# A stick-breaking attention in which the slices of the gates' projection are placed by each step's own columns, not by a fixed period

## The chip, the cores and the metric

One core of a Trainium2 chip runs the whole program. The metric is the device time of one execution in microseconds (us). Engines by their short names: TensorE is PE, VectorE is DVE, ScalarE is ACT, GpSimd is POOL, SyncE is SP (here it only issues transfers).

## What is computed

One inference step of a hybrid decoder for two groups: a prompt of 1024 tokens and 8 samples of 8 tokens each with 256 cached ones. A retention layer comes first, then shared keys and values, then one layer of stick-breaking attention with 16 heads of 64, whose part of the reference is:

```
def sb_layer(h, pos, k_all, v_all, k_pos, w_in, q_g, bias, w_out):
    q, g = jnp.split(h @ w_in, 2, axis=-1)
    q = rmsnorm(q.reshape(B, L, SB_HEADS, SB_DH), q_g)
    o = stick_breaking(q, k_all, v_all, pos, k_pos, bias).reshape(B, L, SB_W)
    return (jax.nn.silu(g) * o) @ w_out

# inside stick_breaking, for each block of 128 queries
z = jnp.einsum('bqhd,bkhd->bhqk', qi, k).astype(F32) * scale + bias_f
log_keep = jnp.where(mask, jax.nn.log_sigmoid(-z), 0.0)
tail = lax.cumsum(log_keep, axis=3, reverse=True)
w = jnp.where(mask, jnp.exp(jax.nn.log_sigmoid(z) + tail_excl), 0.0)
out = jnp.einsum('bhqk,bkhd->bqhd', w, v)
```

The gate g needs a product of its own, `h @ w_in` for 1024 columns. Half of it is made before attention, the other half (columns 512 to 1023) during it. That second half is what the change moves.

## The kernel before

The program has stages that follow each other: opening, retention heads, the product behind them, shared keys and values with queries, attention, output. The change touches the function `attention` alone.

**Pieces.** Heads go in 8 pairs, a pair's queries in 8 blocks of 128. Each of these 64 units is cut into pieces of at most 512 columns of keys (of one head, or of both where 256 columns or fewer are left); 8 further pieces belong to the sample group, one for each sample. That makes 168 pieces, `NPC`; `HALF` is 80, half of the 160 without samples.

**Steps.** Every engine runs its own loop over the pieces p = 0 to 167, a step each. PE in step p: the score of piece p+1 into one of two banks of `z` (L1785, L1786; it waits until the second sigmoid of piece p-1 is done, semaphore `sticks`), then slices (first half of the step), the transposes of piece p-3 (L1795), the attends of the pieces that `batches` lists for this step (L1821), then slices again (second half). ACT in step p: two sigmoids of piece p, `pa_keep` and `pa_take` (L1932), a copy of the transposed piece p-3 for two pieces in three (L1943), and, where a tile of gates ends in step p, the tile's sigmoid, `open_gates` (L1977), for which it waits. DVE: the scan of piece p-1 (L2044), every third copy (L2053), the gate of finished units, and a tile's last product, `finish_gates` (L2122). POOL: the multiplication of piece p (L1722), and two steps after the end of a tile its store, `store_gates` (L1702).

**Slices.** The half product has nine tiles: eight for the prompt and tile 8 for the samples. Each has eight slices of three matmuls with 512 columns (L2980 to L2982; two, L3002 and L3003, for the samples), 72 in all, all into the one bank `pa_acc`. So a tile's first slice waits until DVE has finished the tile before it (`g_ready`). How many slices are done before each half of a step is said by `slices_before(p, part)`: five before the loop, one more in each of the first steps, and from step 4 on eight in six steps (12 halves) of every eight, none in the last two:

```
if p < FIRST_SLOT:
    return min(KD, START + p + (part > 0))
q = 2 * (p - FIRST_SLOT) + (part > 0)
return min(SLICES, KD + KD * (q // PERIOD) + min(KD, (q % PERIOD) * KD // FILL))
```

**What hangs on the end of the tiles.** `steps_done_at(p)` lists the tiles that end in step p, and `G_END` is the step in which tile 8 ends. From it come the opening of the sample gates (PE turns them at G_END+2, DVE copies them at G_END+3, POOL stores them in its step G_END+2), POOL's clearing of `sa_q_diag` at G_END+3 and, on SP at step G_END+1, `load_samples`: the page table, eight loads of the samples' inputs (three of new rows, head rows, bias, `hidden`, two masks; semaphore `inputs_s`), then the first pages of keys and values.

**What does not hang on it.** PE turns the samples' new queries in step 74 (`new_slots` begins at HALF-6) and waits there for all eight inputs (L1748). SP loads the gates of pair 4, `load_g(4)` (L1623), in its step 67, since `g_slots` counts from the end of a pair:

```
def load_g(pair):
    if pair >= 2:
        sp.wait_ge(stored[pair % 2], 16 * (pair // 2))
    if pair == PAIRS // 2:
        for n in range(2):
            sp.wait_ge(g_stored[n], 16 * len(range(n, NT, 2)))
```

Pairs 4 to 7 use the columns that the slices make, so pair 4 waits for the stores of all nine tiles. SP works through its steps in order, and whatever it waits for holds back all that stands behind.

Of the kernel before, what the change touches and what calls it, by code (L numbers as in the profile page):

```python
# [23 lines left out]
P = 128  # L24
D = 1024
KD = D // P
# [64 lines left out]
def build_program(nc, t_in, t_out):  # L91
    ctx = ExitStack()
    with ctx:
        persist = Persistent(nc, ctx, t_in)
        banks = ExitStack()
        at = nc.sbuf_base
        with ExitStack() as joined:
            hw_sem, rt_sem, ro_sem, kq_sem = semaphores(nc, joined, "hw", "rt", "ro", "kq")
            with ExitStack() as layer:
                h = Modulated(nc, layer)  # L100
                head = HeadWeights(nc, hw_sem("w_loaded"))
                opening(nc, t_in, persist, h, head)
                block = joined.enter_context(nc.Block(no_gpsimd_drain=True))
                first = FirstWeights(nc, "ro", t_in["ret_w_out"][0], H * DV // P)
                ahead = RetainedAhead(nc, at, banks.enter_context(nc.psum_tensor("rt_acc", [P, 2, NB], F32)), first)
                kept = retention_heads(nc, t_in, t_out, persist, h, head, first, ahead, block, rt_sem)
            late = ExitStack()
            late_sem = semaphores(nc, late, "pa")
            with ExitStack() as middle:
                pairs = PairBuffers(nc)  # L110
                rated = middle.enter_context(nc.sbuf_tensor("rated", [P, 3, NT], F32))
                x = middle.enter_context(nc.sbuf_tensor("x", [P, NT, D], F32))
                proj = Projection(nc)
                kq_stored = [late_sem(name) for name in ("kq_stored0", "kq_stored1", "kq_last_stored", "kq_parts0", "kq_parts1", "kq_parts_k")]
                with banks:
                    handed = retained_out(nc, t_in, persist, first, x, rated, proj, ahead, kept, block, ro_sem)
                shared_kv_and_queries(nc, t_in, t_out, persist, x, rated, proj, pairs, kq_stored, handed, block, kq_sem)
        first = FirstWeights(nc, "ao", t_in["sb_w_out"][0], KD)
        sa = SampleBuffers(nc, proj.kept)
        held = Held(nc, sa, pairs, ctx.enter_context(nc.psum_tensor("z", [P, 2, NB], F32)))  # L120
        attention(nc, t_in, t_out, persist, proj, first, sa, held, pairs, kq_stored, late, late_sem)
        output(nc, t_in, t_out, persist, first, sa, held)
# [1254 lines left out]
def attention(nc, t_in, t_out, ps, proj, first, sa, held, pairs, kq_stored, ctx, sem):  # L1377


    with ctx:  # L1380
# [11 lines left out]
        pieces = []  # L1392
        for u in range(UNITS):
            wide = (where(u)[1] + 1) * P
            spans = [(NB, wide - NB), (0, NB)] if wide > NB else [(0, wide)]
# [3 lines left out]
        HALF = len(pieces) // 2  # L1399
        at = HALF + 13 - 9  # L1400
# [5 lines left out]
        NPC = len(pieces)  # L1406
# [42 lines left out]
        LAG, TR, WR, KR = 3, 5, 5, 3  # L1449
# [50 lines left out]


        SLICES = NT * KD
        START, FIRST_SLOT, PERIOD, FILL = KD - 3, 4, 16, 12

        def slices_before(p, part):

            if p < FIRST_SLOT:
                return min(KD, START + p + (part > 0))
            q = 2 * (p - FIRST_SLOT) + (part > 0)
            return min(SLICES, KD + KD * (q // PERIOD) + min(KD, (q % PERIOD) * KD // FILL))  # L1510

        def steps_done_at(p):

            begun = slices_before(p, 0) if p else 0
            return [t for t in range(NT) if begun < (t + 1) * KD <= slices_before(p + 1, 0)]
# [60 lines left out]
            else:  # L1576
                engine.wait_ge(w_taken_a, len([n for n in range(p + 1) if not on_vector(n)]))

        batches, held_back = {}, []
        for p, at in enumerate(pieces):  # L1580
            if at.b is not None and held_back:
                batches[held_back[-1] + LAG + 1] = held_back
                held_back = []
            if at.closes:
                held_back = held_back + [p]
            if at.b is not None or len(held_back) == (2 if p < HALF else 1) or at.closes and at.last and at.u % 4 == 3:
                batches[p + LAG + 1] = held_back
                held_back = []
        attend_step = {p: step for step, batch in batches.items() for p in batch}
        gate_step = {attend_step[ends[u]] + 1: u for u in range(3, UNITS, 4)}  # L1590
        assert len(attend_step) == sums_done(NPC - 1) and len(gate_step) == UNITS // 4
# [148 lines left out]
        def _(pe):  # L1740
# [134 lines left out]
            for p in range(NPC):  # L1875
                if p + 1 < NPC:
                    score(p + 1)
                if p in new_slots:
                    turn_new(new_slots[p])
                if p in page_slots:  # L1880
                    turn_pages(*page_slots[p])
                project(slices_before(p, 0), slices_before(p, 1))
                if p >= LAG:
                    turn_w(p - LAG)
                for q in batches.get(p, ()):
                    attend(q)
                project(slices_before(p, 1), slices_before(p + 1, 0))
                if p == G_END + 2:
                    turn_gates()
                if sample_before(p, LAG + 3) is not None:  # L1890
                    fold(sample_before(p, LAG + 3))
# [1365 lines left out]
```

## Time and profile before

| | |
|---|---|
| median of 3 runs | 1812.44 us (1810.49 to 1814.74) |
| the profiled execution | 1811.87 us, its span in the trace 1810.2 us |
| PE busy | 1758.1 us, 97% of the span |
| DVE, ACT, POOL busy | 969.4, 778.2, 267.0 us |
| granted PE clock, mean of the span | 0.995 |
| attention, from its first score to its last | 1362.6 to 1700.4 us |

The table's rows are shares of one profiled execution. PE's busy time counts each matmul to its modelled end, so it overlaps a little with what follows; the clock is given as a share of 2.4 GHz. Where an engine's idle time ends, the trace names the instruction that released it.

### The profile page before, as it was taken

The numbers are of one execution on the slowest core, as the hardware profiler recorded it, in microseconds if no ns is written. First come the engines' busy times: TensorE is split into PE (matmuls) and PEld (weight loads), VectorE is DVE, ScalarE is ACT, GpSimd is POOL, SyncE is SP. The second block draws the span as 40 slices with busy tenths as digits, with TensorE's granted clock in tenths as the row PEclk, the third lists the DMA queues.
The fourth block names the chain that finished last, engine by engine and source line by source line (L and its number), as shares of the span: only waits on it lengthen the run. The fifth ranks groups of instructions, "written<-read, shape, count | busy, mean of one in ns | idle before, by whom it ended". The sixth has DMA issues, their size and how long they took to land. (4 is left out here: it accounts for less than half of the span.)

```text
span 1810.2 us, 27358 instructions
## 1 busy us (share of the span) xinstructions
PE 1758.1 (97%) x9783; PEld 1388.7 (77%) x9783; DVE 969.4 (54%) x1867; ACT 778.2 (43%) x1683; POOL 267.0 (15%) x324
## 2 busy tenths in 40 slices
PE   5999999999999999999999999999998998999998
PEld 2678787878787878777788877788887777677677
DVE  4653535454444444453645554676625667777762
ACT  3742323232323232331434433353326768888720
POOL 2000000000000000000000011101113545555300
PEclk9999999999999999999999999999999999999999
DMA  9231312122222222366433578423365449696252
GB/s 338 87 97 60 95 61 89 67 79 76 75 80 68 87 61 93 104 209 217 130 84 116 190 231 271 157 80 112 102 186 134 123 117 251 194 236 190 86 192 93
DMA packets 153898, 240.60 MB, mean 133 GB/s; under 512 B 13289, under 2 KB 102177, under 8 KB 152770
## 3 DMA queue, kind: packets, MB, share of 16 engines
q1 hardware_dynamic: 136778, 179.69, 33.5%
q0 software_dynamic: 17024, 59.66, 9.3%
q8 instruction: 57, 0.93, 0.2%
q14 instruction: 39, 0.31, 0.1%
HBM read 177.91 MB, written 61.42 MB: 132 GB/s over the span
## 5 line engine op out<-in xcount | busy, mean ns | idle before, releaser
L488 PE MATMUL rt_acc<-rt_w_hi,rt_h_hi 128*128 128x512 f32 x504 | 203.3, 403 | 1.0 <-DVE rt_h_lo L1030 1.0
L490 PE MATMUL rt_acc<-rt_w_hi,rt_h_lo 128*128 128x512 f32 x504 | 197.1, 391 | 0.0
L489 PE MATMUL rt_acc<-rt_w_lo,rt_h_hi 128*128 128x512 f32 x504 | 196.5, 390 | 0.0
L1722 POOL TENSOR_TENSOR pa_take<-pa_take,pa_after_key 128x512 f32<-128x512 f32 (+2 forms) x152 | 153.3, 1011 | 141.7 <-DVE pa_after_key L2044 137.8
L1073 DVE TENSOR_TENSOR rt_by_cos<-rt_raw,rt_cos 128x256 f32<-128x256 f32 (+1 forms) x72 | 30.5, 424 | 243.9 <-ACT rt_raw L903 243.9
L914 ACT COPY rt_qk_t<-rt_tr 128x256 f32<-128x256 f32 (+1 forms) x72 | 26.0, 361 | 278.4 <-PE rt_tr L722 278.4
L2992 PE MATMUL kq_acc<-kq_w_hi,kq_h 128*128 128x512 f32 x320 | 128.6, 402 | 0.0
L2995 PE MATMUL kq_acc<-kq_w_hi,kq_h 128*128 128x512 f32 x320 | 125.1, 391 | 0.0
L2993 PE MATMUL kq_acc<-kq_w_lo,kq_h 128*128 128x512 f32 x320 | 124.7, 390 | 0.0
L1932 ACT ACTIVATE pa_keep<-z,pa_bias 128x128 f32<-128x128 f32 (+3 forms) x192 | 111.1, 600 | 5.9 <-PE z L1786 5.7
L1932 ACT ACTIVATE pa_take<-z,pa_bias 128x128 f32<-128x128 f32 (+3 forms) x192 | 111.1, 603 | 0.0
L490 PEld LDWEIGHTS rt_acc<-rt_w_hi,rt_h_lo 128*128 128x128 f32 x504 | 94.6, 188 | 20.6
L488 PEld LDWEIGHTS rt_acc<-rt_w_hi,rt_h_hi 128*128 128x128 f32 x504 | 94.8, 188 | 19.1 <-DVE rt_h_lo L1030 1.4
L489 PEld LDWEIGHTS rt_acc<-rt_w_lo,rt_h_hi 128*128 128x128 f32 x504 | 94.9, 188 | 17.9 <-issue 0.2
L780 PE MATMUL rt_acc_g<-rt_h_hi,rt_g_hi 128*128 128x512 f32 x256 | 105.6, 413 | 0.0
L2044 DVE TENSOR_TENSOR_SCAN pa_after_key<-pa_keep,pa_eye 128x384 f32<-128x384 f32 (+3 forms) x112 | 93.2, 850 | 19.5 <-POOL pa_take L1722 8.5
L782 PE MATMUL rt_acc_g<-rt_h_lo,rt_g_hi 128*128 128x512 f32 x256 | 100.1, 391 | 0.0
L781 PE MATMUL rt_acc_g<-rt_h_hi,rt_g_lo 128*128 128x512 f32 x256 | 100.1, 391 | 0.0
L1795 PE MATMUL pa_wt<-ident,pa_take 128*128 128x128 f32 x592 | 93.1, 275 | 2.6 <-POOL pa_take L1722 1.4
L1785 PE MATMUL z<-pa_k_t,pa_q_hi 128*128 128x128 f32 (+3 forms) x192 | 76.4, 406 | 16.0 <-ACT pa_take L1932 12.5
L1795 PEld LDWEIGHTS pa_wt<-ident,pa_take 128*128 128x128 f32 x592 | 70.9, 140 | 22.1 <-POOL pa_take L1722 6.7
L2044 DVE TENSOR_TENSOR_SCAN pa_after_key<-pa_keep,pa_after_key,pa_eye 128x512 f32<-128x512 f32 x64 | 81.7, 1276 | 7.4 <-ACT pa_keep L1932 4.0
(406 smaller groups left out, 4025.8 us busy)
## 6 DMA issues: line engine op xcount, KB each, us to landing
ro_a_raw<-retained SPq DMA_DIRECT2D x14, 1024.0 KB, 6.0
rt_w_raw<-in_ret_w_in SPq DMA_DIRECT2D x16, 512.0 KB, 5.2
rt_w_raw<-in_ret_w_in SPq DMA_DIRECT2D x8, 1024.0 KB, 7.8
rt_old<-in_state_ret SPq DMA_DIRECT2D x8, 1024.0 KB, 5.9
rt_g_raw<-in_ret_w_in SPq DMA_DIRECT2D x8, 1024.0 KB, 5.2
out_st_sample<-rt_new POOLq DMA_DIRECT2D x8, 1024.0 KB, 7.9
k_cols<-kq_parts POOLq DMA_DIRECT2D x16, 512.0 KB, 4.0
kq_w_raw<-in_sb_w_in SPq DMA_DIRECT2D x4, 2048.0 KB, 10.2
```

Of the source, the lines that this page charges most:

```text
L488: nc.tensor.matmul(dst, h_hi[:, k, cols], w_hi[:, k, :], start=k == 0, stop=False)
L489: nc.tensor.matmul(dst, h_hi[:, k, cols], w_lo[:, k, :], start=False, stop=False)
L490: last = nc.tensor.matmul(dst, h_lo[:, k, cols], w_hi[:, k, :], start=False, stop=k == KD - 1)
L780: nc.tensor.matmul(dst, g_hi[:, k, part], h_hi[:, k, cols], start=k == 0, stop=False)
L781: nc.tensor.matmul(dst, g_lo[:, k, part], h_hi[:, k, cols], start=False, stop=False)
L1722: nc.gpsimd.tensor_tensor(own, own, later, ALU.mult).then_inc(weighed, 1)
L1795: last = nc.tensor.transpose(dst[:, b * P:(b + 1) * P], take(p)[:, b * P:(b + 1) * P], ps.ident[:])
L1932: last = nc.scalar.activation(dst[:, cols], z[:, p % 2, cols], ACT.Sigmoid, scale=(2 * part - 1) * DH ** -0.5, bias=shift)
L2044: nc.vector.tensor_tensor_scan(ring[:, c0:c0 + n][:, ::-1], k[:, ::-1], opening, seed, ALU.mult, join).then_inc(scanned, 1)
L2992: nc.tensor.matmul(dst, hi, w_hi, start=k == 0, stop=False)
L2993: last = nc.tensor.matmul(dst, hi, w_lo, start=False, stop=t == NPT and k == KD - 1)
L2995: last = nc.tensor.matmul(dst, proj.lo(t)[:, k, :], w_hi, start=False, stop=k == KD - 1)
```

## The change

The constants of the period go. A new function, `spread_slices`, makes a list `cuts` of how many slices are done before each half step, and `slices_before` reads it. For each step it adds up columns: `own_work` is what PE has of its own (the next score, the transposes, the attends, with a charge of 110 for each round of them), `fed_work` what ACT has (two sigmoids of each scan at nine quarters a column, with rounds). A slice counts 690. In a step's second half as many slices are due as keep PE's sum in proportion to ACT's; in its first half one, if any is due by then. At most two are laid in a half, never past the end of a tile, and for three halves after a tile's end none (`PAUSE`). All are done by step 69 (`LEVEL` is 70). The table `batches` is computed earlier, since `own_work` reads it; its rule is the same.

```
-        START, FIRST_SLOT, PERIOD, FILL = KD - 3, 4, 16, 12
+        START, PAUSE, LEVEL = KD - 3, 3, 7 * HALF // 8
+        ROUND, SHARE = 110, 690
...
+        def own_work(p):
+
+            work = 0
+            if p + 1 < NPC:
+                work += ROUND + 7 * pieces[p + 1].wide // 8
+            if p >= LAG:
+                work += 7 * pieces[p - LAG].wide // 8
+            spans = [pieces[q].n // P for q in batches.get(p, ()) if pieces[q].b is None]
+            return work + sum(2 * P * n * 7 // 8 for n in spans) + (2 * ROUND if spans else 0)
+
+        def fed_work(p):
+
+            return 2 * ROUND * pieces[p].scans + 9 * pieces[p].wide // 4 + ROUND
+
+        fed = [sum(fed_work(q) for q in range(p + 1)) for p in range(LEVEL)]
+        owned_by = [sum(own_work(q) for q in range(p + 1)) for p in range(LEVEL)]
+        to_spread = owned_by[-1] + SHARE * (SLICES - START)
+
+        def spread_slices():
+
+            cuts, done, free_at = [START], START, 0
+            for p in range(LEVEL):
+                for part in range(2):
...
+                    goal = START + (fed[p] * to_spread // fed[-1] - owned_by[p]) // SHARE if part else done + 1
+                    if part == 0 and START + (fed[p] * to_spread // fed[-1] - owned_by[p]) // SHARE <= done:
+                        goal = done
+                    goal = SLICES if p == LEVEL - 1 and part else goal
+                    edge = (done // KD + 1) * KD
+                    if 2 * p + part < free_at:
+                        goal = done
+                    goal = max(done, min(goal, done + 2, edge, SLICES))
+                    if goal == edge and goal > done:
+                        free_at = 2 * p + part + 1 + PAUSE
+                    done = goal
+                    cuts.append(done)
+            return cuts
+
+        cuts = spread_slices()

         def slices_before(p, part):

-            if p < FIRST_SLOT:
-                return min(KD, START + p + (part > 0))
-            q = 2 * (p - FIRST_SLOT) + (part > 0)
-            return min(SLICES, KD + KD * (q // PERIOD) + min(KD, (q % PERIOD) * KD // FILL))
+            return cuts[min(2 * p + (part > 0), len(cuts) - 1)]
```

Worked out from the two rules, for steps 1 to 73:

| | before | after |
|---|---|---|
| tile 0 to 8 ends in step (1: first half, 2: second half) | 2 (1), 9 (2), 17 (2), 25 (2), 33 (2), 41 (2), 49 (2), 57 (2), 65 (2) | 1 (2), 7 (1), 16 (1), 25 (1), 33 (2), 44 (1), 51 (1), 61 (1), 69 (2) |
| steps without slices and without attends | 3, 10, 11, 18, 26, 35, 42, 50, 51, 58, 66, 68, 69, 70, 72, 73 | 2, 8, 17, 24, 26, 32, 60, 62, 70, 72, 73 |
| steps with attends and without slices | 19, 27, 34, 43, 59, 67, 71 | 12, 15, 19, 23, 31, 34, 37, 41, 43, 45, 49, 52, 55, 59, 67, 71 |
| `G_END` | 65 | 69 |

The line numbers of the function's later parts grow by 37 in the changed kernel (L1785 becomes L1822, L2980 becomes L3017).

The order on PE, steps 10 and 11 (`z` rows are a score, `pa_acc` rows a slice, `pa_wt` rows the transposes). Before, from the score of piece 11 that opens step 10 to the score that opens step 12:

```order
L1785 MATMUL z<-pa_k_t_3429,pa_q_hi_3430 128x512
L1786 MATMUL z<-pa_k_t_3429,pa_q_lo_3434 128x512
L1795 MATMUL pa_wt<-ident,pa_take 128x128 x4
L1785 MATMUL z<-pa_k_t_3429,pa_q_hi_3430 128x384
L1786 MATMUL z<-pa_k_t_3429,pa_q_lo_3434 128x384
L1795 MATMUL pa_wt<-ident,pa_take 128x128 x4
L1785 MATMUL z<-pa_k_t_3429,pa_q_hi_3430 128x384
L1786 MATMUL z<-pa_k_t_3429,pa_q_lo_3434 128x384
```

After, from the same score to the one that opens step 11:

```order
L1822 MATMUL z<-pa_k_t_3429,pa_q_hi_3430 128x512
L1823 MATMUL z<-pa_k_t_3429,pa_q_lo_3434 128x512
L3017 MATMUL pa_acc<-kq_h,kq_w_hi_3439 128x512
L3018 MATMUL pa_acc<-kq_h,kq_w_lo_3440 128x512
L3019 MATMUL pa_acc<-kq_h,kq_w_hi_3439 128x512
L1832 MATMUL pa_wt<-ident,pa_take 128x128 x4
L3017 MATMUL pa_acc<-kq_h,kq_w_hi_3439 128x512
L3018 MATMUL pa_acc<-kq_h,kq_w_lo_3440 128x512
L3019 MATMUL pa_acc<-kq_h,kq_w_hi_3439 128x512
L1822 MATMUL z<-pa_k_t_3429,pa_q_hi_3430 128x384
L1823 MATMUL z<-pa_k_t_3429,pa_q_lo_3434 128x384
```

Step 10 had no slice and has two now, one before its transposes and one behind them; step 11, whose score is the last pair of rows, had none either and has one.

The order on SP, around the loads that its steps 64 to 70 issue (`pa_v` is `load_v(4)`, `pa_g_t` is `load_g(4)`, `sa_pages` to `sa_by_group` are the page table and the eight input loads of `load_samples`). Before:

```order
L1615 DMA pa_v<-out_v_prompt 128x8x128
L1626 DMA sa_pages<-in_page_table 1x16
L1629 DMA sa_new_rows<-q_rows 64x1024
L1629 DMA sa_new_rows<-out_k_sample 64x1024
L1629 DMA sa_new_rows<-out_v_sample 64x1024
L1630 DMA pa_head_rows<-in_head_rows 16x128
L1631 DMA sa_bias_col<-in_sb_bias 16x1
L1633 DMA sa_hidden<-in_hidden_s 128x1024
L1633 DMA sa_own_block<-in_own_block 128x4
L1633 DMA sa_by_group<-in_by_group 128x32
```

and behind the last page of values, before the loads of the next pair:

```order
L1303 DMA sa_v_pages<-in_cache_v 128x1024
L1623 DMA pa_g_t<-g_cols 128x1024
L1342 DMA pa_k_t<-k_cols 64x1024
L1343 DMA pa_q_hi<-q_cols 64x1024
L1344 DMA pa_q_lo<-q_cols 64x1024
```

After:

```order
L1652 DMA pa_v<-out_v_prompt 128x8x128
L1660 DMA pa_g_t<-g_cols 128x1024
L1663 DMA sa_pages<-in_page_table 1x16
L1666 DMA sa_new_rows<-q_rows 64x1024
L1666 DMA sa_new_rows<-out_k_sample 64x1024
L1666 DMA sa_new_rows<-out_v_sample 64x1024
L1667 DMA pa_head_rows<-in_head_rows 16x128
L1668 DMA sa_bias_col<-in_sb_bias 16x1
L1670 DMA sa_hidden<-in_hidden_s 128x1024
L1670 DMA sa_own_block<-in_own_block 128x4
L1670 DMA sa_by_group<-in_by_group 128x32
```

`load_g(4)` stood behind the whole of `load_samples`, pages included; it stands ahead of it now, because `load_samples` moved from step 66 to step 70 and `load_g(4)` stayed in step 67. The other orders on SP are unchanged.

## Rows read from the trace of the kernel before

**Rows 1.** The page's table of busy time: us, share of the span, instructions.

```profile
PE 1758.1 (97%) x9783; PEld 1388.7 (77%) x9783; DVE 969.4 (54%) x1867; ACT 778.2 (43%) x1683; POOL 267.0 (15%) x324
```

**Rows 2.** Windows of attention: start to end, length, then the header's columns.

```profile
core 0: us, PE busy (x) PEld busy (x) DVE busy (x) ACT busy (x) POOL busy (x), PEclk, DMA share, GB/s
1362.60:1366.50 3.90, 3.90 (x13) 3.13 (x14) 1.36 (x6) 2.43 (x5) 0.31 (x1) 0.57 0.65 214
...
1373.30:1508.20 134.90, 127.69 (x986) 104.19 (x987) 90.65 (x107) 96.34 (x194) 68.91 (x73) 1.00 0.55 130
1508.20:1531.00 22.80, 19.35 (x177) 15.04 (x176) 17.92 (x22) 18.98 (x39) 13.45 (x14) 1.00 1.02 325
```

**Rows 3.** Waits of PE, 1372 to 1500: us, times, longest.

```profile
PE z L1785 <- ACT pa_take L1932: 7.9, 9, 1.1
```

**Rows 4.** Waits of ACT, 1372 to 1500.

```profile
ACT pa_g_out L1977 <- PE pa_acc L2982: 7.4, 6, 2.2
```

**Rows 5.** Timeline of PE, steps 8 to 11: start, us, operation, [idle before].

```profile
1382.49 0.60 PE L1795 MATMUL pa_wt<-ident,pa_take 128*128 128x128 f32 x4
1382.85 0.48 PE L1785 MATMUL z<-pa_k_t,pa_q_hi 128*128 128x512 f32 x1
...
1384.40 1.75 PE L1821 MATMUL pa_out<-pa_w_t,pa_v 128*64 128x128 f32 x28
...
1386.65 0.39 PE L2982 MATMUL pa_acc<-kq_h,kq_w_hi 128*128 128x512 f32 x1
...
1387.34 0.60 PE L1795 MATMUL pa_wt<-ident,pa_take 128*128 128x128 f32 x4
1388.88 0.45 PE L1785 MATMUL z<-pa_k_t,pa_q_hi 128*128 128x384 f32 x1 [0.95 <-ACT pa_take L1932]
```

**Rows 6.** Timeline of PE, steps 65 to 74.

```profile
1507.98 0.40 PE L3003 MATMUL pa_acc<-kq_w_lo,kq_h_s 128*128 128x512 f32 x1
...
1511.69 0.39 PE L1785 MATMUL z<-pa_k_t,pa_q_hi 128*128 128x256 f32 x1 [2.33 <-ACT pa_take L1932]
...
1517.77 0.33 PE L1785 MATMUL z<-pa_k_t,pa_q_hi 128*128 128x128 f32 x1 [0.84 <-ACT pa_take L1932]
...
1524.46 0.71 PE L1748 MATMUL pa_wt<-ident,sa_new_rows 64*128 64x64 f32 x8
```

**Rows 7.** Timeline of SP's issues, from `load_samples` to `load_g(4)`.

```profile
1508.41 0.24 SPq L1626 DMA_DIRECT2D sa_pages<-in_page_table  x1
...
1512.50 0.43 SPq L1633 DMA_DIRECT2D sa_by_group<-in_by_group  x1
...
1520.75 1.42 SPq L1303 DMA_DIRECT2D sa_v_pages<-in_cache_v  x2
1523.97 0.34 SPq L1623 DMA_DIRECT2D pa_g_t<-g_cols  x1
```

**Rows 8.** Timeline of DVE, the copy of the turned sample gates.

```profile
1515.25 0.40 DVE L2126 COPY pa_g_out<-pa_acc 128x256 f32<-128x256 f32 x1
```

**Rows 9.** Timeline of POOL, the store of the sample gates.

```profile
1516.71 0.81 POOL L1702 DMA_DIRECT2D g_cols<-pa_g_out  x1
```

**Rows 10.** Transfers issued 1516 to 1517.5: count, KB each, us to landing.

```profile
sa_v_pages<-in_cache_v SPq DMA_DIRECT2D x2, 512.0 KB, 8.1
g_cols<-pa_g_out POOLq DMA_DIRECT2D x1, 128.0 KB, 7.2
```

**Rows 11.** Transfers issued 1481 to 1482.5, a quiet time.

```profile
g_cols<-pa_g_out POOLq DMA_DIRECT2D x1, 256.0 KB, 2.4
```

**Rows 12.** Transfers issued 1508 to 1513.5, the last of the inputs.

```profile
sa_by_group<-in_by_group SPq DMA_DIRECT2D x1, 16.0 KB, 6.8
```

**Rows 13.** Timeline of PE, the first scores and slices of attention.

```profile
1362.59 0.30 PE L1785 MATMUL z<-pa_k_t,pa_q_hi 128*128 128x128 f32 x1 [2.96 <-PEq L57]
...
1363.47 0.63 PE L2981 MATMUL pa_acc<-kq_h,kq_w_lo 128*128 128x512 f32 x1
1363.90 0.63 PE L2982 MATMUL pa_acc<-kq_h,kq_w_hi 128*128 128x512 f32 x1
...
1366.75 0.39 PE L2980 MATMUL pa_acc<-kq_h,kq_w_hi 128*128 128x512 f32 x1
```

More of the change, by code:

```diff
@@ L1502, in attention @@
         SLICES = NT * KD
-        START, FIRST_SLOT, PERIOD, FILL = KD - 3, 4, 16, 12
+        START, PAUSE, LEVEL = KD - 3, 3, 7 * HALF // 8
+        ROUND, SHARE = 110, 690
+        batches, held_back = {}, []
+        for p, at in enumerate(pieces):
+            if at.b is not None and held_back:
+                batches[held_back[-1] + LAG + 1] = held_back
+                held_back = []
+            if at.closes:
+                held_back = held_back + [p]
+            if at.b is not None or len(held_back) == (2 if p < HALF else 1) or at.closes and at.last and at.u % 4 == 3:
+                batches[p + LAG + 1] = held_back
+                held_back = []
@@ new lines, in attention @@
+        fed = [sum(fed_work(q) for q in range(p + 1)) for p in range(LEVEL)]
[5 more added lines that the diff above has]
+                for part in range(2):
+                    behind = owned_by[p - 1] if p and not part else owned_by[p] if part else 0
+                    goal = START + (fed[p] * to_spread // fed[-1] - owned_by[p]) // SHARE if part else done + 1
[11 more added lines that the diff above has]
+            return cuts
@@ L1577, in wait_taken @@
                 engine.wait_ge(w_taken_a, len([n for n in range(p + 1) if not on_vector(n)]))
[L1579 to L1588, printed above, removed]
         attend_step = {p: step for step, batch in batches.items() for p in batch}
```

## The prediction, made before the changed kernel was run

> **What bounds the kernel now.** I read the busy table of the page first. TensorE (PE) is busy for 97% of the span [rows 1], so a change of order can give back only its idle time. The stretches of attention come next. Steps 4 to 65, which carry the gates' slices, last 134.9 us with PE busy 127.7 of them; the 22.8 us behind them, in which the slices have ended and the sample group is being opened, are worse covered, 19.35 us [rows 2]. The list of waits says what PE waits for while slices run: in steps 4 to 60 it is one thing, 9 times, the second sigmoid of a piece (`pa_take`) on ScalarE (ACT), 7.9 us in all and at most 1.1 [rows 3]. Score of piece p+1 may not start before the sigmoids of piece p-1 have left `z`.
>
> Where do the nine stand? The timeline at the end of tile 1 shows it. Attends of step 9 run for 1.7 us from 1384.40, then comes the tile's last slice, whose last matmul starts at 1386.65. ACT has to open that tile before its next sticks, so it stands until then; six such waits cost it 7.4 us [rows 4]. PE meanwhile enters steps 10 and 11, which hold neither a slice nor attends, only a score and four transposes. It runs through the first faster than ACT through two sigmoids, and waits 0.95 us before the score that opens step 11 [rows 5], and again behind that. I call such a step bare. From the table of steps in the text on the change, the order of before has ten bare steps among 3 to 60 and nine of them are followed by a wait. The matmul before a wait is drawn to its modelled end (0.60 us from 1387.34, for four transposes; the same four from 1382.49 let the next score in after 0.36 [rows 5]), so a wait costs PE 0.24 more than its number: 7.9 + 9 x 0.24 = **10.1 us** for nine.
>
> **The change, term by term.** Each of the 72 slices is still done once, with the same instructions, and no engine gets work that it had not. Only their place changes, so these are the terms.
>
> *1. Waits between slices.* After the change the bare steps among 2 to 62 are 2, 8, 17, 24, 26, 32, 60 and 62: eight, not ten. The pairs 10, 11 and 50, 51 are gone. Six of nine tiles now end in a step's first half, ahead of transposes that ACT waits for anyway, so ACT's 7.4 us of standing shrinks too. That is not what decides, since a bare step is short for ACT whatever came before it. By the rate of before (nine waits for ten bare steps, 10.1 / 9 = 1.12 us each) eight bare steps give 8 x 0.9 x 1.12 = 8.1 us: gain 2.0 us. Bounds: none of it, or all 10.1 us. I take the rate, as it is the nearest.
>
> *2. Steps 66 to 69.* Before, the last slice is in step 65; steps 66, 68 and 69 are bare. PE waits 2.33 us behind step 66, because ACT stands in the opening of the sample tile, and 0.84 behind step 69 [rows 6]. Now the slices reach to step 69. The 2.33 moves with the sample tile's end to step 70; the 0.84 (1.1 with the 0.24) goes. Gain 1.1 us.
>
> *3. The sample inputs are late.* This is the largest term, and it lies on SP, not on PE. SP issues `load_samples` at step `G_END + 1`, where G_END is the step that ends tile 8. It moves from step 66 to step 70. `load_g(4)` stays at step 67, and for this pair alone it waits until all nine gate stores have landed, the one of tile 8 too. Before, it stood behind the sample loads, and its wait until 1523.97 stopped nobody [rows 7]. Now it stands in front of them: the order on SP shows `pa_g_t` directly ahead of `sa_pages`. PE's first transpose of the sample rows stays in step 74 and waits for all eight input loads.
> Take M as the end of the last slice (before: its last matmul starts at 1507.98 [rows 6], M = 1508.2). The chain from M: merge, sigmoid, transposes, and VectorE's (DVE) copy of the turned gates, which starts 1515.25 and takes 0.40 [rows 8]; GpSimd (POOL) issues the store at 1516.71, M + 8.5 [rows 9]. It landed after 7.2 us, while SP was sending for pages [rows 7, 10]; an earlier store of gates in a quiet time landed after 2.4 [rows 11]. Now SP has nothing under way then, so I take 2.4 and keep 7.2 as the far end: M + 10.9. Then SP issues `load_g(4)`, 0.5 us with its queue: M + 11.4. From the first sample load (1508.41) to the issue of the last input (1512.50) are 4.1 us [rows 7], and this last landed after 6.8 [rows 12]: 10.9 in all, so the inputs are there at **M + 22.3**; with a landing of 2.4 instead of 6.8 at M + 17.9.
> When does PE want them? From the start of step 70 (1517.77) to the first sample transpose (1524.46) PE goes 6.7 us without waiting [rows 6]. With the 2.33 + 0.24 of term 2 it is there at M + 9.3. So it waits 22.3 - 9.3 = **13.0 us**. Ends: 17.9 - 9.3 = 8.6, and 13.0 + 4.8 = 17.8 if the store takes 7.2 again. Nothing covers this: everything behind step 74 on PE is queued behind the wait, DVE and ACT need the turned pieces, and POOL needs DVE. When it ends, the others have caught up, but the short waits of the sample opening behind it hang on chains that start at that transpose.
>
> *4. The clock after the pause.* The granted clock falls where PE has stood. Before attention it stands for 2.96 us; then two neighbouring matmuls of the first slices start 0.43 us apart (1363.47, 1363.90), against 0.23 from 1366.75 on [rows 13], and the mean clock of that stretch reads 0.57 [rows 2]: 1.2 GHz for most of it. From 1363.06, where they begin, to 1366.75 are nine matmuls, so some 8 x 0.2 = 1.6 us were lost. A pause four times as long should bring the same once: cost 1.6 us; ends 0 (steps 75 to 77 already wait for ACT and DVE) and 3.2 for twice that.
>
> **Sum:** -2.0 - 1.1 + 13.0 + 1.6 = +11.5 us. The profiled execution took 1811.87 us (span 1810.2), so 1823.4; the median of the runs is 0.57 above it, and 1811.87 + 11.5 + 0.57 gives **1824.0 us**.
>
> The Trainium skill speaks on the store in term 3 ("DMA: Bandwidth & Descriptors", Specifications): pieces under 512 bytes don't run at line rate, because the engine reads and rewrites. The sample gates' store has rows of 64 numbers, 256 bytes, while the quiet store that I priced it by has rows of 2 KB. By that page the 2.4 us would be too little; with the far end of 7.2 the sum would be 16.3 and the time 1828.8. The row alone, 7.2 us, doesn't part the size of the pieces from the traffic.
> On the clock the skill ("TensorE: Matmul & The Clock Gate", Why this matters for your kernels) advises against idle gaps between bursts, and this speaks against the change. Rows 13 agree; the sum would be the same by rule and by row.
>
> **Rivals.**
> *A. Even spreading takes away all of ACT's waits.* Every step would then be longer than ACT's two sigmoids and a copy. For it: PE's work in these steps exceeds ACT's on average (127.7 against 96.3 us busy [rows 2]). Against it: eight bare steps are left. It gives -10.1 - 1.1 + 13.0 + 1.6 = +3.4 us, 1815.8. Chance 0.05, within the measurement's 0.2% (3.6 us, about what a measurement of this kernel can tell from no change).
> *B. Faster.* The loads of the samples are not late: either SP passes the wait of `load_g(4)` early, or PE reaches the transposes after the inputs. It decides if the inputs are there before M + 9.3. Then terms 3 and 4 vanish: -3.1 us, 1809.3; with A's full gain 1801.2. For it: before, PE never waited for an input there. Against it: the store that SP now waits for is not even issued before M + 8.5 by rows 8 and 9. Chance 0.03.
> *C. More is late.* The store takes its 7.2 us and the clock needs twice as long: -3.1 + 17.8 + 3.2 = +17.9, 1830.3; the key pages, issued behind the inputs, might add a wait in step 78. SP issues the pages right behind the inputs, and PE has four steps to do before it turns them, so I price none. Chance 0.07.
> *D. Nothing moves in time* because the order is only arithmetic on the same work. The ordered lists speak against it. It is in the 0.05 of A.
>
> **How the numbers follow.** Forecast 0.85, A (with D) 0.05, B 0.03, C 0.07. The forecast's own ends: 8.6 us of wait, 3.1 gained and no loss by the clock give +5.5, 1817.9; 17.8 with 1.6 and 3.1 gives +16.3, 1828.8. The range 1817 to 1830 takes in both and most of C. Faster by over 0.2% has B's 0.03, within 0.2% A's 0.05, slower the other 0.92.
>
> **What would show it.** SP issues `pa_g_t` before `sa_pages`, some 3 us after POOL's last `g_cols` (term 3's first half). PE shows one wait of 9 to 18 us before the first transpose of `sa_new_rows`, the longest of attention. The clock reads half behind it. Between steps 4 and 62 PE's waits for `pa_take` add up to 6 to 8 us, against 7.9. From step 80 on the steps last as before. It would be wrong if that one wait is under 5 us, or if the waits for `pa_take` fall under 2 us.

## The result, and the profile after

The changed kernel takes 1823.78 us, median of five runs (1822.44 to 1827.83), against 1810.58 for the kernel before (five runs, 1810.49 to 1814.74). The ratio is 1.0066, 95% interval 1.0049 to 1.0083: 8.9 to 15.0 us slower. The forecast was 1824.0, range 1817 to 1830.

The profiled execution has a span of 1823.0 us against 1810.2, a difference of 12.8. From its page, the span and the busy table:

```profile
span 1823.0 us, 27358 instructions
...
PE 1761.5 (97%) x9783; PEld 1392.7 (76%) x9783; DVE 969.9 (53%) x1867; ACT 777.2 (43%) x1683; POOL 266.8 (15%) x324
```

The instructions and the 97% are those of [rows 1]. The busy time of PE grew by 3.4 us with as many matmuls, so some of them ran slower; the rest of the 12.8 is idle time. Below are PE's waits over attention's slices and the opening of the samples (1362 to 1560): total us, times, longest. The kernel before has no entry like the second:

```profile
PE z L1822 <- ACT pa_take L1969: 11.6, 12, 2.4
PE pa_wt L1785 <- DMA sa_by_group<-in_by_group: 11.6, 1, 11.6
```

Who held that load back stands in SP's waits and issues of the same stretch. The waits of SP, and then its timeline (L1659 is the wait in `load_g(4)` for the gate stores, L1652 a load of values, L1663 to L1670 `load_samples`):

```profile
SPq L1659 <- DMA g_cols<-pa_g_out: 23.9, 1, 23.9
```

```profile
1501.34 0.39 SPq L1652 DMA_DIRECT2D pa_v<-out_v_prompt  x1
1525.70 0.33 SPq L1660 DMA_DIRECT2D pa_g_t<-g_cols  x1
1526.07 0.29 SPq L1663 DMA_DIRECT2D sa_pages<-in_page_table  x1
...
1530.20 0.43 SPq L1670 DMA_DIRECT2D sa_by_group<-in_by_group  x1
```

SP stands for 23.9 us and issues nothing between 1501.34 and 1525.70. The nine loads of the samples need no gates at all, yet they are issued behind the wait. The first one leaves at 1526.07, against 1508.41 before [rows 7]. The wait ends with the store of tile 8, in POOL's timeline and in the list of transfers issued from 1522 to 1534 (KB each, us to landing):

```profile
1523.20 0.81 POOL L1739 DMA_DIRECT2D g_cols<-pa_g_out  x1 [3.33 <-DVE pa_g_out L2163]
```

```profile
g_cols<-pa_g_out POOLq DMA_DIRECT2D x1, 128.0 KB, 2.4
...
sa_by_group<-in_by_group SPq DMA_DIRECT2D x1, 16.0 KB, 4.8
```

PE's timeline from the last slice to step 77 shows what became of these 12 us:

```profile
1512.07 0.40 PE L3040 MATMUL pa_acc<-kq_w_lo,kq_h_s 128*128 128x512 f32 x1
...
1515.90 0.50 PE L1822 MATMUL z<-pa_k_t,pa_q_hi 128*128 128x512 f32 x1 [2.42 <-ACT pa_take L1969]
...
1517.45 2.91 PE L1858 MATMUL pa_out<-pa_w_t,pa_v 128*64 128x128 f32 x28
...
1535.05 1.11 PE L1785 MATMUL pa_wt<-ident,sa_new_rows 64*128 64x64 f32 x8 [11.55 <-DMA sa_by_group<-in_by_group]
...
1543.23 0.39 PE L1822 MATMUL z<-pa_k_t,pa_q_hi 128*128 128x256 f32 x1
```

The same pieces of before, for comparison: the score that opens step 71, its attends, and the score in step 77.

```profile
1518.93 0.50 PE L1785 MATMUL z<-pa_k_t,pa_q_hi 128*128 128x512 f32 x1
...
1520.03 1.75 PE L1821 MATMUL pa_out<-pa_w_t,pa_v 128*64 128x128 f32 x28
...
1530.30 0.39 PE L1785 MATMUL z<-pa_k_t,pa_q_hi 128*128 128x256 f32 x1
```

The 28 matmuls of step 71's attends are the same work in both, and take 2.91 us instead of 1.75. The windows of the three parts (steps 71 to 73, the wait, and the steps behind it) show the granted clock, PEclk, in the last column but two:

```profile
core 0: us, PE busy (x) PEld busy (x) DVE busy (x) ACT busy (x) POOL busy (x), PEclk, DMA share, GB/s
1515.90:1523.30 7.40, 7.38 (x52) 5.93 (x52) 4.26 (x7) 4.98 (x12) 2.88 (x4) 0.77 0.00 0
1523.30:1535.00 11.70, 0.20 (x1) 0.00 (x0) 3.29 (x3) 1.23 (x3) 5.64 (x5) 0.65 0.77 207
1535.00:1543.20 8.20, 7.92 (x56) 6.12 (x56) 1.46 (x2) 4.15 (x8) 0.00 (x0) 0.67 1.03 408
```

Means between 0.5 and 1.0 say that half clock (1.2 GHz) held for a part of each. There are two stretches of it, one from just behind PE's pause of 2.42 us, one that begins within the pause of 11.55 and goes on behind it. Laid along PE's timeline, the 12.8 us of the span are:

| stretch | before | after | difference |
|---|---|---|---|
| start to attention's first score | 1362.59 | 1361.62 | -1.0 |
| first score to the start of step 71 | 156.34 | 154.28 | -2.1 |
| steps 71 to 73, to the first sample transpose or the wait | 5.53 | 7.43 | +1.9 |
| the wait for the sample inputs | 0 | 11.7 | +11.7 |
| from there to the score in step 77 | 5.84 | 8.18 | +2.3 |
| the rest, to the end | | | about 0 |

The first line is code that the change doesn't touch. In the thirteen profiles of this study attention's first score began anywhere between 1360.34 and 1363.19, so a difference of 1 us there says nothing. The second line is firmer: three further profiles with the slices of the change (experiments 1 and 3 and the busy wait of 4) took 154.3 to 154.4 us there. The fourth, the change itself in experiment 4, took 155.7; its mean clock over 1362 to 1373 was 0.69, where the others have 0.84 to 0.89.

### The profile page after: what moved, and what is told of

It reads as the page before. It is cut to its first block and busy times, and to the rows that moved or that the text cites. A ratio compares the mean times of both kernels' runs of the same rounds, so it can differ in the third digit from the quotient of the medians.

```text
span 1823.0 us, 27358 instructions
## 1 busy us (share of the span) xinstructions
PE 1761.5 (97%) x9783; PEld 1392.7 (76%) x9783; DVE 969.9 (53%) x1867; ACT 777.2 (43%) x1683; POOL 266.8 (15%) x324
## 5 line engine op out<-in xcount | busy, mean ns | idle before, releaser
L1822 PE MATMUL z<-pa_k_t,pa_q_hi 128*128 128x128 f32 (+3 forms) x192 | 77.8, 414 | 15.9 <-ACT pa_take L1969 12.6
```

## The experiments

Each kernel differs from the changed kernel or from the one before by one constant or a few lines. Times are medians; a ratio is against the kernel before in runs beside it, its 95% interval in brackets, and a difference in us is that ratio taken of 1810.6. `M` is the end of the last slice, the gates of pair 4 are what `load_g(4)` loads, and a bare step is one without slices and without attends.

**1. Only SP's order put back.** In the changed kernel, `load_g(4)` moves from step 67 to step 71, so it stands behind `load_samples` again:

```
-            g_slots = {ends[NPT * pair - 1] + 8: pair + 1 for pair in range(1, PAIRS - 1)}
+            g_slots = {ends[NPT * pair - 1] + (12 if pair == 3 else 8): pair + 1 for pair in range(1, PAIRS - 1)}
```

> The change with one edit: SP loads the gates of pair 4 at step 71 in place of 67, so behind the sample loads of step 70, as it was before. My theory (the one wait of 11.6 us comes from SP standing in load_g(4) ahead of the sample loads): the first sample load is issued 0.2 us after the last slice, the inputs land 9 to 11 us after it, PE asks for them after 9.3 to 11, so the wait falls to under 2 us and the half clock behind it goes: 1823.8 - 11.7 - 2.3 plus 0 to 1.8, that is 1809.8 to 1811.6 us. Rival (the loads are late because they start at step 70 at all, or are slow by themselves): a wait of 6 us or more stays, over 1816 us.

Measured: 1812.02 us, ratio 1.0000 (0.9990 to 1.0009). SP and PE in their timelines:

```profile
1511.84 0.24 SPq L1663 DMA_DIRECT2D sa_pages<-in_page_table  x1
...
1530.77 0.33 SPq L1660 DMA_DIRECT2D pa_g_t<-g_cols  x1
```

```profile
1523.93 0.71 PE L1785 MATMUL pa_wt<-ident,sa_new_rows 64*128 64x64 f32 x8
```

The first sample load is issued 0.2 us behind M, and the first sample transpose has no wait in front. The slices lie as in the change, and the loss is gone: it came from one position in SP's list. Against the kernel before, the new places of the slices are worth nothing that can be measured here. Half clock still came twice, behind a pause of 2.41 us and in steps 77 to 79, where PE had no late input to wait for. There it took 11.63 us from the first sample transpose to that of the key pages, where the kernel before took 10.08. PE's timeline and the window:

```profile
1531.71 1.09 PE L1832 MATMUL pa_wt<-ident,pa_take 128*128 128x128 f32 x4 [1.21 <-DVE sa_bias L2098]
```

```profile
1531.70:1535.00 3.30, 3.29 (x24) 2.70 (x24) 2.19 (x5) 2.06 (x5) 1.26 (x2) 0.50 0.53 159
```

The kernel before has a pause of 1.20 us in the same place and keeps the full clock.

**2. Only SP's order of the change, in the kernel before.** The same line with `6` for pair 3 puts `load_g(4)` ahead of `load_samples`; the slices stay as they were.

> The kernel before with one edit: SP loads the gates of pair 4 at step 65, ahead of the sample loads of step 66; no slice moves. My theory: the store of tile 8 is issued 8.5 us after the last slice (1508.2) and lands 2.4 later, the first sample load then at 1519.5, the last input there at 1519.5 + 4.1 + 4.9 = 1528.5, PE asks at 1524.5: a wait of 4 us before the first transpose of sa_new_rows, and up to 1.6 us of half clock: 1810.6 + 4 to 5.6, 1814.6 to 1816.2 us. Rival (what costs is the place of the slices, not the order on SP): no such wait, 1810.6 us.

Measured: 1818.74 us, ratio 1.0032 (1.0021 to 1.0044), +5.8 us. PE's waits from 1362 to 1560, and SP's timeline:

```profile
PE pa_wt L1748 <- DMA sa_by_group<-in_by_group: 2.9, 1, 2.9
```

```profile
1520.14 0.33 SPq L1623 DMA_DIRECT2D pa_g_t<-g_cols  x1
1520.51 0.29 SPq L1626 DMA_DIRECT2D sa_pages<-in_page_table  x1
```

The swap alone makes the wait, but a short one. `load_g(4)` leaves at M + 11.6, against M + 13.4 in the change, and here PE has steps 66 to 73 to do behind the last slice, and in the change only 70 to 73. So the loss of the change needs both halves: the swap on SP, and an end of the slices four steps nearer to step 74. The time is longer than the 1814.6 to 1816.2 expected, because half clock came twice: behind a pause of 2.35 us, and again from 1.2 us behind the end of the wait. The second time cost as much as in experiment 1 (11.63 us for 10.08), where there is no such wait, so it isn't shown that the wait of 2.9 us brought it.

**3. PE kept busy while it waits.** In the change, 110 transposes of the identity matrix are issued ahead of the wait for the inputs, into columns that the next transposes overwrite. They add work and change nothing of the result.

```
-                if n == 0:
-                    pe.wait_ge(inputs_s, 16 * 8)
...
+                if n == 0:
+                    for _ in range(110):
+                        nc.tensor.transpose(dst[:, 0:P], ps.ident[:], ps.ident[:])
+                    pe.wait_ge(inputs_s, 16 * 8)
```

> The change with 110 transposes of the identity put before PE's wait for the sample inputs, into the bank that the next transposes write anyway. They fill about 9.7 of the 11.7 us in which PE stood. My theory (the 2.3 us lost between steps 74 and 77 is the half clock behind the pause): the wait shrinks to about 2 us, the clock stays full behind it, and the time falls by 2.3 us against the change, to 1821.5. Rival (those steps are slow for another reason, such as transfers or the other engines' queues running dry): they still take 8.2 us, and the time stays at 1823.8.

Measured: 1825.71 us (ratio 1.0072, 1.0056 to 1.0089). PE's timeline, then the window behind the wait:

```profile
1524.95 12.17 PE L1783 MATMUL pa_wt<-ident 128*128 128x128 f32 x110
1538.10 0.71 PE L1787 MATMUL pa_wt<-ident,sa_new_rows 64*128 64x64 f32 x8 [0.97 <-DMA sa_by_group<-in_by_group]
```

```profile
1538.10:1545.80 7.70, 6.34 (x60) 4.85 (x60) 3.20 (x7) 5.59 (x11) 1.46 (x2) 1.00 1.03 407
```

The clock reads 1.00 behind the busy wait. From the first sample transpose to that of the key pages it is 10.08 us, as in the kernel before, against 12.42 in the change: the 2.3 us behind the wait are the clock. But the whole was no faster, and the 1821.5 us expected were missed. The store of tile 8 landed after 3.2 us instead of 2.4, the last input after 5.5 instead of 4.8, and the part behind attention's last score is 0.9 us longer.

**4. The same two again, side by side.** The change as it is:

> The changed kernel once more, unedited, beside the next run on the same chip. It tells how far two profiles of one kernel differ in the chain behind the last slice: the sample inputs at 22 to 24 us after it, the first transpose of sa_new_rows to the first transpose of key pages in 12.4 us (10.1 with full clock), 1823 to 1825 us in all.

and the busy wait:

> The run with 110 transposes in the wait once more, now beside the change itself. In its first run the steps behind the wait took 10.1 us in place of 12.4, as my theory of the clock says, but the inputs landed 24.2 us after the last slice in place of 22.7, and the attention began 1.6 us later. Theory 1 (those two are chance): inputs at 22 to 24 us as in the run beside it, the time 1 to 2.5 us below it. Theory 2 (PE's transposes slow the transfers down): inputs 1.4 us later than in the run beside it again, and the time within 1 us of it.

Measured: 1825.47 for the change (ratio 1.0071, 1.0054 to 1.0088), 1824.53 for the busy wait (1.0062, 1.0046 to 1.0079). The steps behind the wait took 12.06 and 10.08 us, so that part repeats. The total differs by 0.9 us, just under the 1 to 2.5 expected of the first theory, and the two intervals overlap. Inputs were there at M + 23.9 and M + 23.7, so the later inputs of experiment 3 didn't repeat as a difference. Two smaller things did repeat with the added transposes: the store of tile 8 landed after 3.1 us, against 2.4 beside it, and the end behind attention's last score was 0.7 us longer (110.4 against 109.7 us). Why, no run here shows.

**5. The slices end four steps sooner.** The change with `LEVEL` 66 for 70: the same rule of columns, with all slices done by step 65 as in the kernel before.

> The change with LEVEL 66 in place of 70: the same rule lays the slices, but ends them in step 65 as before, so the sample loads are at step 66, ahead of load_g(4). My theory: no late inputs; bare steps (no slice, no attends) among 2 to 62 are 2, 7, 20, 32, 53 and 58, six in place of ten, and at 1.12 us for nine in ten of them 4 x 0.9 x 1.12 = 4.0 us are gained: 1806.6 us. Rival 1 (the placement by columns gives only what it gave in the change, 2.1 us): 1808.5. Rival 2 (denser slices make another engine or the clock the bound): 1810.6 or more.

Measured: 1806.55 us, ratio 0.9964 (0.9949 to 0.9978), -6.5 us, as expected. PE's waits from 1366 to 1503:

```profile
PE z L1822 <- ACT pa_take L1969: 2.9, 5, 1.3
```

In the kernel before it is 7.9 us in 9 waits there, and 8.5 in 9 in the change. Of steps 2 to 62 six are bare, instead of eight in the change and ten before.

**6 and 7. The period of before with another filling.** `FILL` 12 became 14 (seven of eight steps get slices, and four of steps 2 to 62 are bare) and 10 (five of eight get slices, and fourteen are bare).

> The kernel before with FILL 14 in place of 12: a tile's eight slices lie in seven of eight steps. Bare steps among 2 to 62 are then 3, 11, 35 and 51, four in place of ten; the last slice is in step 66. My theory (a bare step costs PE 0.9 x 1.12 us whatever rule lays the slices): 6 x 1.0 = 6 us gained, 1804.6 us. Rival (the waits follow the ends of tiles, where ACT stands for a last slice; there are as many of them as before): within 1 us of 1810.6.

> The kernel before with FILL 10 in place of 12: slices in five steps, none in three. Bare steps among 2 to 62 are 3, 10, 11, 17, 18, 25, 26, 33, 35, 42, 50, 51, 57 and 58, fourteen in place of ten. My theory: 4 x 1.0 = 4 us lost, 1814.6 us. Rival (waits follow the ends of tiles): within 1 us of 1810.6.

Measured: 1807.72 (ratio 0.9971, 0.9959 to 0.9982) and 1814.98 (1.0018, 1.0008 to 1.0027): -5.2 and +3.3 us, where -6 and +4 were expected. So `FILL` 14, one constant of the old rule, can't be told apart from `LEVEL` 66 of the new one: the intervals overlap. PE's waits from 1366 to 1503, first for 14, then for 10:

```profile
PE z L1785 <- ACT pa_take L1932: 4.8, 7, 1.1
```

```profile
PE z L1785 <- ACT pa_take L1932: 7.3, 10, 0.9
```

The sign is that of the count of bare steps both times: six fewer bring 5.2 us, four more cost 3.3. But the waits don't carry the second result. At 10 they list 7.3 us (and 0.8 for POOL), no more than the 7.9 of before, and the kernel is slower all the same, by 3.5 us up to the first sample transpose. Part of it is a stretch at half clock behind a pause of 2.20 us, which the kernel before doesn't have (shown in the last section); the rest stands in no list. And at 14 there are seven waits for four bare steps, so waits stand behind steps with work of their own as well.

**8. `LEVEL` 68.** Six bare steps; the slices end in step 66, so `load_samples` is in step 67, still ahead of `load_g(4)`.

> The change with LEVEL 68 in place of 70: the last slice is in step 66, first half, so the sample loads are in SP's step 67, where they still stand ahead of load_g(4). Six bare steps among 2 to 62 (2, 7, 13, 20, 32, 58), and one fewer behind them. My theory: no late inputs, 4.0 us gained in 2 to 62 and up to 1 behind: 1805.6 to 1806.6 us. Rival (a later end of the slices makes the inputs late in any order on SP): 1810 us or more.

Measured: 1805.12 us (1804.08 to 1805.28), ratio 0.9959 (0.9945 to 0.9973), -7.4 us, 0.5 below the range expected. It is faster than the kernel before and than the change. PE's waits from 1366 to 1503, then its timeline where the other kernels have the pause of 2.3 to 2.4 us:

```profile
PE z L1822 <- ACT pa_take L1969: 3.3, 7, 1.3
```

```profile
1507.24 0.50 PE L1822 MATMUL z<-pa_k_t,pa_q_hi 128*128 128x512 f32 x1 [0.91 <-ACT pa_take L1969]
...
1510.58 0.33 PE L1822 MATMUL z<-pa_k_t,pa_q_hi 128*128 128x128 f32 x1 [0.35 <-ACT pa_take L1969]
```

The pause is split into 0.91, 0.36 and 0.35 us here, and the clock stays full.

**9 and 10. `LEVEL` 69**, alone and with the edit of experiment 1. Here the slices end in step 68. It is the first value of `LEVEL` at which `load_samples` comes behind `load_g(4)`.

> The change with LEVEL 69: one more than in the run with 68 (1805.1 us), which moves the last slice from step 66 to step 68 and so the sample loads from SP's step 67 to its step 69, behind load_g(4). My theory (a cliff by SP's order): inputs 22.7 us after the last slice, PE there some 12 us after it, a wait of 10 to 11 us and 2.3 us of half clock: 1805.1 + 10.5 + 2.3 = 1817.9 us. Rival (each later step of the last slice costs about the same): between 1805.1 and the change's 1823.8 at half way, 1814 us, and no wait over 8 us.

> LEVEL 69 and the gates of pair 4 loaded by SP at step 71. My theory: no late inputs, the last slice's place costs nothing by itself: 1804 to 1807 us. Rival: over 1810 us.

Measured: 1819.39 (1.0034, 1.0021 to 1.0047) and 1809.63 (0.9982, 0.9973 to 0.9992). PE's waits (1362 to 1560) of the first, and SP's timelines of the first and of the second:

```profile
PE pa_wt L1785 <- DMA sa_by_group<-in_by_group: 7.2, 1, 7.2
```

```profile
1518.42 0.34 SPq L1660 DMA_DIRECT2D pa_g_t<-g_cols  x1
1518.80 0.29 SPq L1663 DMA_DIRECT2D sa_pages<-in_page_table  x1
```

```profile
1509.87 0.25 SPq L1663 DMA_DIRECT2D sa_pages<-in_page_table  x1
...
1523.73 0.33 SPq L1660 DMA_DIRECT2D pa_g_t<-g_cols  x1
```

From `LEVEL` 68 to 69 the time jumps by 14 us, and 9.8 of them go when one load is put behind the others. The wait is 7.2 us rather than the 10 to 11 expected. Half clock behind it (13.31 us to the key pages' transpose instead of 10.08) and behind a pause of 2.40 us makes up for that. The second was expected at 1804 to 1807 and missed: it lists 5.0 us of waits between slices instead of the 3.3 of `LEVEL` 68, and it has the pause of 2.40 us in one piece with half clock behind it, which `LEVEL` 68 doesn't have.

## Why the prediction was right, point by point

**Term 3, the late inputs, carried it.** Forecast 13.0 us, measured 11.7. Both links of the chain were seen in advance. SP stood at `load_g(4)` until the last store landed; experiment 1 takes that away with one line, and 12 us go with it. And PE had too few steps left to cover it; experiment 2 has the first link without the second, and a wait of 2.9. Inside the term two sizes were off and nearly cancelled. The chain from M to the store's issue took 10.9 us, not 8.5: on DVE a copy of a transposed piece now stands ahead of the gates' copy and waits 2.95 us for PE, and PE's half clock fell in that time. The store then landed in 2.4 us, as taken, in both profiles of the change, and the far end of 7.2 didn't come. The same store took 7.0 us in experiment 1, where the samples' pages are under way beside it again, so the long landing goes with the traffic and not with the store itself. The Trainium skill ("DMA: Bandwidth & Descriptors", Specifications) says that transfers in pieces under 512 bytes don't run at line rate. These traces show no price for that: 128 KB in rows of 256 bytes landed in the 2.4 us that 256 KB in rows of 2 KB took [rows 11]. As it is half the bytes, a small price could hide in it. The loads took 4.5 us from the issue of `load_g(4)` to that of the last input, and this one 4.8 to land instead of 6.8. So the inputs were there at M + 22.7, against a forecast of 22.3. PE stood there at M + 11.0 instead of 9.3, because it ran steps 71 to 73 at half clock. With the inputs 0.4 later and PE 1.7 later the wait is 1.3 us shorter.

**Term 4, the clock, was half seen.** Behind the long wait it cost 2.3 us, against 1.6 taken, and experiments 3 and 4 show that this is the clock and not late inputs of other engines: with PE busy through the wait the same stretch takes the 10.08 us of before. What was not seen is the other stretch, 1.9 us in steps 71 to 73 behind the pause of 2.42 us. Before, the pause of 2.33 us at the same kind of place left the clock full. As a sum the clock cost 4.2 us where 1.6 was taken. But the 1.9 lay in front of the wait: it brought PE later to the wait, and the store's chain ran through it too, so how much of it is in the total isn't shown.

**Terms 1 and 2, the gains, were too large.** Forecast -2.0 and -1.1, together -3.1; measured -2.1. PE's listed waits in 1372 to 1503 are 8.5 us in 9, where 6 to 8 were forecast and 7.9 in 9 stood before. So the test that the prediction set itself for term 1 was missed. The rate of before failed in both of its parts. Before, all nine waits stand behind bare steps and last 0.6 to 1.1 us. In the change only five of the eight bare steps (2, 8, 17, 26 and 62) have a wait behind them, but these five last 1.3 to 1.4 us each, and four more, of 0.2 to 0.8 us, stand behind steps that hold work (14, 45, 51 and 54). Here is the wait behind step 26:

```profile
1424.17 0.39 PE L1822 MATMUL z<-pa_k_t,pa_q_hi 128*128 128x256 f32 x1 [1.43 <-ACT pa_take L1969]
```

```profile
PE z L1822 <- ACT pa_take L1969: 8.5, 9, 1.4
```

ACT's standing for the last slices of tiles did nearly go, from 7.4 us [rows 4] to 0.5, as the order had said. But it moved to another line: ACT now stands longer for PE's transposes. Its waits over 1372 to 1503, before and then in the change:

```profile
ACT pa_w_t L1943 <- PE pa_wt L1795: 27.0, 23, 2.5
```

```profile
ACT pa_w_t L1980 <- PE pa_wt L1832: 34.5, 29, 2.8
ACT pa_g_out L2014 <- PE pa_acc L3019: 0.5, 1, 0.5
```

With a small third entry (1.8 and 0.5) ACT stood 36.2 us in all before and 35.5 in the change, so it was hardly ever free sooner.

The count of bare steps is a rough rule and no more. It gave the sign in four further orders (experiments 5 to 8), but one step was worth 0.8 and 0.9 us with `FILL` 10 and 14, and 1.6 and 1.9 with `LEVEL` 66 and 68 (6.5 and 7.4 us for four); and `LEVEL` 69 has as many bare steps, six, as `LEVEL` 68, with 5.0 us of waits in place of 3.3. Where the 2.1 us between first score and step 71 come from isn't settled: the listed waits over that stretch, steps 66 to 70 included, are 11.1 us before and 11.2 in the change. Matmul ends are modelled, and what hides in them is not listed.

**The rivals.** A (all of ACT's waits vanish) fell with the 8.5 us. B (the loads aren't late) fell with M + 22.7 against M + 11.0; experiment 1 is what B's world looks like, at 1812.0 where B had 1809.3. The difference is the half clock, which B left out, and the smaller gain. C (store in 7.2, clock twice) fell on the store; its twice-lost clock was there. D (nothing moves) fell with the result, whose interval begins at +8.9 us.

**The sum.** Forecast -3.1 + 13.0 + 1.6 = +11.5. Along the timeline it is -2.1 + 1.9 + 11.7 + 2.3 = +13.8, less 1.0 in front of attention that belongs to no term: +12.8 by the profiled executions, and +8.9 to +15.0 by the ratio. That 1824.0 lies 0.2 us from the measured 1823.78 is luck in part: the forecast started from 1812.44, a median of three runs, and the median of five is 1810.58. (Its own terms add up to 1823.9.) The step that failed in size is the clock; the step that failed in kind is term 1, whose waits neither became fewer nor shorter in sum.

## What to carry to other kernels

When a change moves where a stage ends, list everything whose place in an in-order queue hangs on that end and everything whose place doesn't, and look for a wait that now stands ahead of loads it has nothing to do with. Here such a wait cost 12 us, one position in a list took it back, and an end of the slices three steps sooner, on the good side of the same edge, made a kernel 7 us faster than the one before.

Then ask what the wait is for. `load_g(4)` fetches rows 512 to 639 and columns 0 to 1023 of `g_cols`. By `store_gates` these are written by tiles 0 and 1, and tile 8 goes into columns behind them. So the load stood for a store that it doesn't read; the one wait covers pairs 5 to 7 as well. This is read from the kernel, and no run tests a wait for fewer tiles.

One entry in a list of waits is not an engine's idle time. ACT's standing for tiles went from 7.4 us to 0.5, its standing in all from 36.2 to 35.5, and PE's waits for it didn't fall.

## What the runs showed of the hardware that was not expected

**Half clock came with pauses of 2.2 to 2.4 us ten times out of eleven.** It began in or shortly behind (at most 1.6 us) a pause of 2.20 to 2.42 us in ten profiles (the change twice, the busy waits, experiments 1, 2, 5, 7, 9 and 10), and not in the kernel before (2.33). In the change it cost the 1.9 us of the table. In the two kernels in which the waiting was split into pieces of 0.35 to 0.91 us, `FILL` 14 and `LEVEL` 68, it didn't fall. But length alone doesn't decide: in experiment 1 it fell again with a pause of 1.21 us, which left it full in other kernels. The windows of the kernel before and, below, of `FILL` 10, in both the stretch behind the pause:

```profile
1511.70:1514.00 2.30, 2.30 (x31) 2.13 (x33) 2.26 (x3) 2.29 (x6) 0.87 (x1) 1.00 1.03 195
```

```profile
1510.30:1512.00 1.70, 1.65 (x7) 1.17 (x8) 1.61 (x2) 1.70 (x4) 0.86 (x1) 0.67 1.17 225
1512.00:1514.00 2.00, 2.00 (x11) 1.88 (x11) 2.00 (x4) 1.07 (x2) 0.88 (x3) 0.50 1.11 210
```

What decides between them is open. The Trainium skill ("TensorE: Matmul & The Clock Gate", Why this matters for your kernels) advises against idle gaps between bursts of matmuls. The wait of 11.55 us, with half clock behind it, agrees; for the short pauses these runs give no rule.

**The long wait cost more than its length.** The 11.7 us at the samples brought 2.3 more behind it. Filling the wait with idle transposes gave those back, but the total was 1.9 us above the first runs of the change and 0.9 below those beside it, and the runs can't tell that from nothing.
